# Three products with an unread sum after the first, third and fifth state step of the first and the last head pair

## What is computed

```python
def step(s, inp):
    r_t, w_t, k_t, v_t, z_t, bb_t = inp
    sz = jnp.einsum("bhij,bhj->bhi", s, z_t)
    s = s * w_t[:, :, None, :] + sz[..., None] * bb_t[:, :, None, :] + v_t[..., None] * k_t[:, :, None, :]
    return s, jnp.einsum("bhij,bhj->bhi", s, r_t)

s0 = jnp.zeros((b_, RWKV_HEADS, RWKV_HEAD, RWKV_HEAD), f32)
_, y = lax.scan(step, s0, (tm(r_h), tm(w_h), tm(k_h), tm(v_h), tm(z_h), tm(b_h)))
```

## Time and profile before

| | |
|---|---|
| median of three timed executions | 1487.45 us |
| the three | 1484.16, 1487.45, 1488.33 us |
| the profiled execution, its own time | 1489.23 us |
| its span, first to last instruction | 1487.4 us |
| mean granted TensorE clock | 0.985 of full speed |
| PE busy | 1451.0 us, 98% of the span |
| DVE, ACT, POOL busy | 827.5, 509.6, 68.9 us |

### The profile page before, as it was taken

One profiled execution on the slowest core, in us unless ns is written; L12 is line 12 of the kernel. 1 busy time (PEld: TensorE's weight loads), 2 busy tenths in 40 slices (PEclk: granted clock), 3 DMA queues, 4 the chain that ended last, 5 costly groups with the idle time before them and its releaser, 6 DMA issues.

```text
span 1487.4 us, 21897 instructions
## 1 busy us (share of the span) xinstructions
PE 1451.0 (98%) x9722; PEld 1196.1 (80%) x9722; DVE 827.5 (56%) x1038; ACT 509.6 (34%) x590; POOL 68.9 (5%) x65
## 2 busy tenths in 40 slices
PE   9999999998999999998999999999998999999997
PEld 6777787777888888887888888888887888888886
DVE  7758686767645354444746454454437545254455
ACT  7545454533312122223344332423433313122222
POOL 0000000013000000001200000000013000000000
PEclk9989999998999999998999999999998999999999
DMA  5202120102323232231222122122121322323221
GB/s 186 72 18 77 31 77 32 72 30 87 126 87 111 85 109 89 89 109 64 86 77 85 57 96 103 58 91 107 57 85 55 130 85 89 110 85 113 85 98 72
DMA packets 19726, 125.61 MB, mean 84 GB/s; under 512 B 2288, under 2 KB 2288, under 8 KB 5808
## 3 DMA queue, kind: packets, MB, share of 16 engines
q1 hardware_dynamic: 19088, 121.29, 22.9%
q0 software_dynamic: 544, 2.91, 0.6%
HBM read 122.10 MB, written 2.10 MB: 83 GB/s over the span
## 4 chain that ended last, share of the span: by engine, by line
PE 93%; DVE 4%; ACT 1%; issue 1%; POOL 0%; DVEq 0%; POOLq 0%
PE bank L342 21%; PE bank L345 20%; PE bank L348 20%; PE bank L546 4%; PE bank L543 4%; PE bank L547 4%; PE bank L1481 2%; PE bank L1478 2%; PE bank L1475 2%; PE bank L793 2%; PE bank L356 1%; PE bank L800 1%; PE bank L1511 1%; PE bank L1510 1%; PE bank L1509 1%
## 5 line engine op out<-in xcount | busy, mean ns | idle before, releaser
L342 PE MATMUL bank<-XH,WH 128*128 128x512 f32 x944 | 379.1, 402 | 14.7 <-DVE XL L435 12.6
L345 PE MATMUL bank<-XL,WH 128*128 128x512 f32 x944 | 370.6, 393 | 0.0
L348 PE MATMUL bank<-XH,WL 128*128 128x512 f32 x944 | 370.6, 393 | 0.0
L315 DVE TENSOR_TENSOR WL<-raw,WH 128x2048 fp32r<-128x2048 f32 (+1 forms) x111 | 249.7, 2251 | 177.4 <-ACT WH L309 177.4
L309 ACT ACTIVATE WH<-raw 128x2048 fp32r<-128x2048 f32 (+1 forms) x111 | 208.2, 1877 | 277.5 <-DMA raw<-weights 277.5
L342 PEld LDWEIGHTS bank<-XH,WH 128*128 128x128 f32 x944 | 179.5, 190 | 59.5 <-issue 20.3
L345 PEld LDWEIGHTS bank<-XL,WH 128*128 128x128 f32 x944 | 179.7, 190 | 37.9 <-issue 1.9
L348 PEld LDWEIGHTS bank<-XH,WL 128*128 128x128 f32 x944 | 179.1, 190 | 38.4
L659 ACT ACTIVATE AH<-relu 128x512 fp32r<-128x512 f32 x64 | 40.5, 633 | 250.0 <-DVE relu L684 250.0
L684 DVE SCALAR_TENSOR_TENSOR relu<-bank,rB 128x512 f32<-128x512 f32 x64 | 44.2, 690 | 100.0 <-PE bank L348 100.0
L342 PE MATMUL bank<-AH,WH 128*128 128x512 f32 x256 | 99.6, 389 | 0.0
(11 more groups left out here) (329 smaller groups left out, 2037.3 us busy)
## 6 DMA issues: line engine op xcount, KB each, us to landing
raw<-weights SPq DMA_DIRECT2D x107, 1024.0 KB, 4.8
raw<-weights SPq DMA_DIRECT2D x8, 512.0 KB, 4.9
h<-x_fm SPq DMA_DIRECT2D x4, 512.0 KB, 8.1
out_tm<-hT SPq DMA_DIRECT2D x8, 256.0 KB, 2.1
rc<-ret_const POOLq DMA_DIRECT2D x1, 1536.0 KB, 6.9
pp<-pairs POOLq DMA_DIRECT2D x4, 199.0 KB, 4.3
cst<-const SPq DMA_DIRECT2D x1, 641.0 KB, 12.0
gain_row<-last_gain POOLq DMA_DIRECT2D x1, 512.0 KB, 3.5
```

The costliest lines, as they stand in the source:

```text
L315: nc.vector.tensor_tensor(WL[i][:, :n], raw[i][:, :n], WH[i][:, :n], ALU.subtract).then_inc(S("w_lo"), 1)
L342: mm = pe.matmul(bank[b][:], wh, xh, start=(k == 0), stop=False)
L345: mm = pe.matmul(bank[b][:], wh, xl, start=False, stop=False)
L348: mm = pe.matmul(bank[b][:], wl, xh, start=False, stop=(k == len(xs) - 1))
```

## The change

In the loop over chunks, after the steps c = 1, 3 and 5 of the pairs that are not in `FILLED` (p = 0 and p = 3), PE issues three more products: the first 128 columns of `XH[:, k, :]` as the stationary tile, all 512 columns of it as the moving one, into bank 0, each as a sum of its own (`start` and `stop` are set). Nothing reads bank 0 afterwards; the next unit that uses it starts a new sum. Ahead of the first three PE waits for the semaphore of bank 0's last reader. In all these are 2 x 3 x 3 = 18 matmuls. No other engine gets, loses or moves an instruction.

```diff
@@ -1047,6 +1047,14 @@
                     over_tokens(c + 1)
                 if c in (3, 5):
                     between(6 + c // 4)
+
+
+
+                if c in (1, 3, 5) and p not in FILLED:
+                    if c == 1:
+                        pe.wait_ge(S("acc_free0"), use.now(0))
+                    for k in range(3):
+                        pe.matmul(bank[0][:], XH[:, k, 0:P], XH[:, k, :], start=True, stop=True)
             mm.then_inc(S("y_heads"), 1)
```

## The result

The changed kernel takes **1494.02 us** (median of 5 executions, 1493.42 to 1495.23) against 1487.45 us (median of 5, 1484.16 to 1488.91). The ratio is 1.0041, with a 95% interval of 1.0023 to 1.0058: slower by 0.2 to 0.6%. I had forecast 1488.0 us and a range that ended at 1493.0. One slow execution of the kernel before, 5129.08 us, among the 31 measured beside f1 to f4, counts in no ratio. A ratio comes with its measurement and is not exactly that of the two medians; differences "by the ratio" are it times the time before.

What follows compares the result with a forecast made beforehand. PE was taken as the bound, busy for 98% of the span and 93% of the last-ending chain. The terms -4.15 and +2.34 in pair 0 and +2.34 in pair 3 gave +0.53 on 1487.45: 1488.0 us, range 1484.5 to 1493.0.

Steps and rivals of the forecast that it cites:

- The price of a group: State steps of pairs 0 and 3: three products cost 0.77 us at full clock, 2.34 us per pair, nothing hidden.
- My 0.80: Step c = 1 of a pair: adding a group there costs 1.79 - 0.99 = 0.80 us.
- I take the median for an execution in which the clock fell: Whole kernel: the median before, 1487.45 us, was taken to include the low clock in pair 0.
- rival 2: Pair 0: the median before has no fall, so both pairs only pay, +4.68 us, 1492.1 us; chance 0.16.
- -4.15 in pair 0: Pair 0: the gain in the sum if the fall of the clock doesn't come at all, 4.15 us.
- The cluster near 1488 and the one at 1484: Timed executions before: times near 1488 read as having the fall, the one 3.3 us below the median as lacking it.
- The same work thus took 13.44 - 9.29 = 4.15 us longer: Pair 0, first L1037 to L823: low clock's cost, against pair 1's stretch without its groups, 4.15 us, all on the path.
- DVE's work moves along: State steps of pair 3: DVE's and ACT's work there starts from the same steps and moves along; no size given.
- Does the change keep the clock?: Pair 0, from 82 to 94 us: yes, more likely than not; gain between 0 and 4.15 us, taken as 4.15.
- The sum: Whole kernel: -4.15 and +2.34 in pair 0, +2.34 in pair 3, together +0.53 us, giving 1488.0 us.
- The rule on idle waits: Pair 0: the skill's rule that long idle waits drop the clock; by it, filling short gaps would not help.
- What's actually happening: Pair 0: skill section saying the chip's watch on PE runs freely; taken to change rival 2's chance, not its price.

Runs made afterwards that it cites:

- f1: The changed kernel with one product in each group instead of three, 6 in all: 1490.95 us, ratio 1.0019 to the kernel before.
- f4: The kernel before, no groups, with DVE making the low part of pair 1's first weight chunk in two halves: 1489.11 us, ratio 1.0002.
- g4: The kernel before, unchanged, run for one more profile: own time 1490.53 us, no fall in pair 0.
- g3: The kernel before, unchanged, run for one more profile: own time 1486.81 us, no fall in pair 0.
- e1: The kernel before with the groups added in pair 0 only: 1490.01 us, ratio 1.0010.
- e3: The change once more, groups in both pairs, against the kernel before: 1493.21 us, ratio 1.0027.
- f2: The changed kernel with six products in each group instead of three, 36 in all: 1496.88 us, ratio 1.0055 to the kernel before.
- f3: The kernel before with only the first group, three products after c = 1 of pair 0: 1489.60 us, ratio 1.0004.
- The long measurement: The run e3: the change measured again over 12 executions against 35 of the kernel before, ratio 1.0027 (1.0015 to 1.0040).
- e0: The kernel before once more, unchanged: 1489.07 us, ratio 1.0001; its profile shows a fall in pair 0.
- g1: The kernel before with unread products in PE's waits at the three norms after a layer, 14 behind the spread, none in the steps: 1493.14 us, ratio 1.0034.
- h1: g1 with six more unread products ahead of the next norm's sums, against the kernel before: 1487.85 us, ratio 1.0001.

## Why the prediction was wrong

**The price of a group** held: 0.77 us by the distance of starts, 1.79 us per step in the changed profile, and linear in the number of products. The first group costs 0.77 too: the step c = 1 took 83.61 - 81.85 = 1.76 us with it and 0.99 without. My 0.80 had set a step c = 3 with a group against a step c = 1 without, so that a pair costs 2.31 us and both 4.6.

**"I take the median for an execution in which the clock fell"** is the step that failed. Three of seven profiles of the kernel before have no fall in pair 0, and the executions around its median have a mean clock (0.986 and more) that none of the four profiles of it with such a fall had. Where it doesn't fall, the groups have nothing to win back and cost their whole 4.6 us: in pair 0 from the stretch of 10.1 to that of 12.37 us, 2.3 us, and the same in pair 3. That was rival 2, with 1492.1 us, which I gave 0.16. The term "-4.15 in pair 0" thus counted for the median what, by the mean clocks, only a minority of the executions has to give. It was not the two levels of time that told it. The cluster near 1488 and the one at 1484 looked like executions with and without a fall, but the profiles with none range from 1486.5 to 1490.5, and those with one from 1489.1 to 1494.6. Other falls come and go as well, at 37 and 362 us, and those at 334 and 700 us vary in length; a fall of 3.4 us at 37 cost 1.6 us (g4 set beside g3). A single profile showed a fall, and I read it as a property of the kernel.

**"The same work thus took 13.44 - 9.29 = 4.15 us longer"** was mis-sized: 3.3 us. The stretch at full clock came from pair 1, which lacks the wait of 0.72 us for the low part of a chunk. The row that would have told it was DVE's L315 right after pair 0's last step; I said that DVE's work moves along, and did not ask what is late next. The remaining 0.1 lies in small differences of the stretches.

**"Does the change keep the clock?"** was right as far as the profiles go: in none of four with all the groups in pair 0 (the changed kernel, e1, e3, f2) did it fall there, nor in the one of f3, against seven of the twelve profiles of kernels with no group there. One product did not keep it (f1). Four profiles are weak evidence: with a fall in four executions of ten, four without one come by chance in 0.13 of cases. The 3.3 us less of low clock in e1 and e3, with an interval clear of zero, are the stronger sign.

**The sum.** With a fall in three executions of ten, the change should cost 4.6 - 0.3 x 3.3 = 3.6 us on average; with a fall in six of ten, 2.6. The long measurement gives 4.0 (interval 2.2 to 6.0 us), the first one 6.1 by the ratio (3.4 to 8.6 us). Both intervals hold 3.6, the first of them barely, and only the long one holds 2.6. The part of the first above this (by the medians 1.6 us are the draw of five executions on each side), and the 3.7 us behind the mixer in the changed profile, I can't put down to the change: e3 doesn't have the fall at 364 us, profiles of the kernel before (e0, g4) do. That the groups shift later falls by moving the work was not tested by itself and stays open.

**The rule on idle waits**: the Trainium skill, TensorE: Matmul & The Clock Gate, "HAM oscillation — how this bites in real kernels", names long idle waits as what takes the clock down. The fall in pair 0 had none; where waits of 4.2 us were filled the falls there were gone in g1's profile, which agrees with it; in h1's, with the same products in these waits, the clock was still low there for 3.4, 3.4 and 6.8 us, in place of 13.7, 10.2 and 6.8 in g3. The same page's "What's actually happening", that the watch on PE runs freely of the kernel, is what seven profiles of one program now agree with: the same code fell at 83, 84 or 85 us, or not at all. I had cited it and let it change a chance only; it should have told me to look at the spread first.

## What to carry to other kernels

A fall of the clock seen in one profile is one draw: before paying for a cure in every execution, count in how many executions it falls, by further profiles and by the mean granted clock of the timed executions, those around the median above all. Unread products cost their issue time unless they lie in a true wait of TensorE, and low clock costs nothing where another engine's chain ends last; so price both at the place, by what waits next. And a stretch taken as the undisturbed reference must have the same waits as the disturbed one, those that the slowness hides too.

## What the hardware showed that I had not expected

- The same program, profiled seven times, had its clock low for 10 to 14 us in pair 0 four times and not at all three times; its executions ranged from 1485.49 to 1494.80 us in one series.
- The clock fell in a stretch in which PE's longest gap was 0.45 us (before) and held in the same stretch with a gap of 0.71 us (g3). The gap alone does not decide it.
- Over 117 executions of one program, time rose by 0.45 us with each us at the low clock, while the 22 us of low clock that h1 removed gained nothing: it depends on the place.
- With a wait filled, the clock fell at the next thin place instead (in the profile of g1, at 361 us): g1 removed 14 us of low clock and lost 5 us; six further products of 0.23 us at each of three places brought these back (h1).
